# Expert values: order of the first loads, spread of the late vectors, and the final norm in PSUM

## The reference, cut to what matters

```python
def _layernorm(x, g, b):
    mu = jnp.mean(xf, axis=-1, keepdims=True)
    var = jnp.mean(jnp.square(xf - mu), axis=-1, keepdims=True)
    y = (xf - mu) * lax.rsqrt(var + NORM_EPS) * g + b
...
        expert = e1 * PEER_NKEYS + e2
        g = jax.nn.softmax(top_s)
        act = jax.nn.gelu(jnp.einsum('thkd,td->thk', u_tab[expert], ht))
        return jnp.einsum('thk,thkd->td', g * act, v_tab[expert])
...
        y_ff = _peer(h, ...)
        x = _layernorm(DEEPNORM_ALPHA * x + (1.0 + g2) * y_ff, ln2_g[l], ln2_b[l])
```

## Time and profile before

| what | us |
|---|---|
| median of three runs (1647.85 to 1650.1) | 1649.09 |
| the profiled execution | 1649.95 |
| its span in the profile | 1648.2 |
| PE busy | 1532.8 (93%) |
| DVE busy | 1287.7 (78%) |
| POOL busy | 957.5 (58%) |
| ACT busy | 686.8 (42%) |

### The profile page before, as it was taken

How to read it: one execution, slowest core, us unless ns; L and a number is a source line. 1 busy time by engine, 2 the same in 40 slices (tenths; PEclk the granted TensorE clock), 3 DMA queues, 4 the chain that set the end, 5 groups by cost and what they waited for, 6 DMA issues and landing times.

```text
span 1648.2 us, 21717 instructions
## 1 busy us (share of the span) xinstructions
PE 1532.8 (93%) x7951; PEld 1275.6 (77%) x7951; DVE 1287.7 (78%) x2005; ACT 686.8 (42%) x1270; POOL 957.5 (58%) x599
## 2 busy tenths in 40 slices
PE   6996898969999999997999999979899999999994
PEld 2344576437899999997999999957788888888883
DVE  5868731373139999999888899259799999999997
ACT  2030463104244343436888888323233333333340
POOL 2620000020026777785777788758789989989863
PEclk9997998989999999998999999989999999999997
DMA  9874206416015777785999999989999999999971
GB/s 369 313 212 52 29 1 213 132 51 204 1 49 172 261 262 263 263 309 196 369 351 380 354 361 378 393 295 360 381 378 379 365 383 372 383 369 377 367 253 51
DMA packets 217110, 438.91 MB, mean 266 GB/s; under 512 B 37156, under 2 KB 129828, under 8 KB 215212
## 3 DMA queue, kind: packets, MB, share of 16 engines
q1 hardware_dynamic: 179420, 302.44, 52.1%
q0 software_dynamic: 36864, 134.23, 22.5%
q10 hardware_dynamic: 720, 0.85, 0.2%
HBM read 379.66 MB, written 56.64 MB: 265 GB/s over the span
## 4 chain that ended last, share of the span: by engine, by line
PE 43%; DVE 18%; DMA 4%; issue 3%; POOL 1%; SPq 1%; ACT 0%; POOLq 0%; DVEq 0%; ACTq 0%
PE ps L1642 9%; PE ps L1643 9%; PE ps L1644 9%; PE ps L1618 5%; PE ps L1620 5%; PE ps L1619 4%; DVE junk L1700 2%; DMA a_in<-act_scr 2%; DMA v_raw<-in_peer_v 1%; PE ps L1633 1%; DVE cand L1737 1%; PE ps L1634 1%; DVE eq L1775 1%; DVE route L1776 1%; DVE idx L1735 1%
## 5 line engine op out<-in xcount | busy, mean ns | idle before, releaser
L1511 POOL TENSOR_TENSOR utl<-u_raw,uth 128x1024 fp32r<-128x1024 f32 x128 | 308.9, 2414 | 240.5 <-ACT uth L1528 238.6
L1618 PE MATMUL ps<-h2h,uth 128*128 128x384 f32 x1024 | 348.0, 340 | 0.2 <-POOL utl L1511 0.2
L1517 POOL TENSOR_TENSOR vl<-v_raw,vh 128x1024 fp32r<-128x1024 f32 x128 | 310.4, 2426 | 63.4 <-ACT vh L1528 61.5
L1620 PE MATMUL ps<-h2h,utl 128*128 128x384 f32 x1024 | 343.0, 335 | 0.0
L1619 PE MATMUL ps<-h2l,uth 128*128 128x384 f32 x1024 | 342.8, 335 | 0.0
L1642 PE MATMUL ps<-vh,wh 128*128 128x512 f32 x768 | 302.4, 394 | 17.9 <-DVE wl L1824 14.3
L1643 PE MATMUL ps<-vl,wh 128*128 128x512 f32 x768 | 301.3, 392 | 0.0
L1644 PE MATMUL ps<-vh,wl 128*128 128x512 f32 x768 | 301.0, 392 | 0.0
L1819 DVE TENSOR_TENSOR w_f<-a_in,g_in 128x384 f32<-128x384 f32 x128 | 231.7, 1811 | 55.5 <-DMA a_in<-act_scr 54.2
L1528 ACT ACTIVATE vh<-v_raw 128x1024 fp32r<-128x1024 f32 x128 | 135.3, 1057 | 198.2 <-DMA v_raw<-in_peer_v 182.4
L1618 PEld LDWEIGHTS ps<-h2h,uth 128*128 128x128 f32 x1024 | 192.9, 188 | 0.5 <-POOL utl L1511 0.5
(11 more groups left out here) (352 smaller groups left out, 2250.8 us busy)
## 6 DMA issues: line engine op xcount, KB each, us to landing
u_raw<-in_peer_uT SPq DMA_DIRECT2D x128, 512.0 KB
v_raw<-in_peer_v SPq DMA_DIRECT2D x128, 512.0 KB
w_ada<-in_w_ada SPq DMA_DIRECT2D x12, 2048.0 KB, 13.3
act_scr<-acts SPq DMA_DIRECT2D x64, 384.0 KB
g_scr<-stage SPq DMA_DIRECT2D x12, 2048.0 KB
g_in<-g_scr SPq DMA_DIRECT2D x32, 768.0 KB
...
```

The source lines that it names most:

```text
L1511: tt(k.utl[b % 3][:, :, :].rearrange(f3), k.u_raw[:, b % 4].rearrange(f3), k.uth[b % 3][:, :, :].bitcast(F32).rearrange(f3), ALU.subtract) ...
L1517: tt(k.vl[:, n % 4], k.v_raw[:, n % 4], k.vh[:, n % 4].bitcast(F32), ALU.subtract).then_inc(k.vl_done, 1)
L1618: mm(o, hi, k.h2h[:, kt, SP:T], start=(kt == 0), stop=False)
L1620: ins = mm(o, lo, k.h2h[:, kt, SP:T], start=False, stop=(kt == DK - 1))
```

## The change

Four things. (1) SP's list at the seam of the two stages: the loads of v blocks 0 and 1 stand in front of the load of u block 127 and of the store of activations 122/123; the second `g_in` stands behind v block 3; the last store of activations (`store_acts(63)`) stands behind the loads of v blocks 4 and 5; from there on each `g_in` is loaded one pair of blocks earlier. (2) `gate2`, `ln2_g`, `ln2_b` and the four tiles of `x1b` are seven loads of 512 KB, after v blocks 33, 41, 49, 57, 65, 73 and 81. (3) The skip and the statistics work in place in PSUM, by halves of 512 columns; those of token tile 0 stand on DVE among v blocks 126 and 127. PE's last four blocks go half by half for the last two tiles and tell each half (`y_done`). (4) For tiles 0 to 2 ACT applies mean and scale from PSUM to `y`, POOL multiplies by `ln2_g` and adds `ln2_b`; tile 3 is finished on DVE in three passes and stored in two halves.

```diff
@@ experts, k.block.sync @@
-        def load_ag(p):
+        def load_g(q):
+            sp.dma_start(k.g_in[:, q % 2]..., k.g_scr[:, :, 4 * q:4 * q + 4]...).then_inc(g_loaded[q % 2], 16)
+
+        def load_a(p):
             if p >= 2:
                 sp.wait_ge(k.w_done, 2 * p - 2)
-            if p % 2 == 0:
-                q = p // 2
-                sp.dma_start(k.g_in[:, q % 2]...)
+                if p % 2 and p < NBLK // 2 - 1:
+                    load_g((p + 1) // 2)
...
-            if b % 2:
+            if b % 2 and b < NBLK - 1:
                 store_acts(b // 2)
             if b in STORE_AT:
                 store_g(STORE_AT[b])
+            if b == NBLK - 6:
+                sp.wait_ge(k.g_out, GROUPS4)
+                load_v(0)
+                load_v(1)
             if b == NBLK - 5:
                 for c in range(2):
                     sp.wait_ge(g_stored[c], 16 * (NCH // 2))
-                sp.wait_ge(k.g_out, GROUPS4)
-                scr = k.mod_scr
-                for p in range(2):
-                    load_ag(p)
-                    load_v(2 * p)
-                    load_v(2 * p + 1)
+                load_g(0)
+                load_a(0)
+                load_v(2)
+                load_a(1)
+                load_v(3)
+                load_g(1)
...
         for p in range(2, NBLK // 2):
-            load_ag(p)
+            load_a(p)
             load_v(2 * p)
             load_v(2 * p + 1)
-            if p == 8:
-                sp.dma_start(k.gate2[:, :], ...).then_inc(s_gate2, 16)
-                sp.wait_ge(k.act_out, NBLK)
-                for name, dst in (("ln2_g", k.ln2_g), ("ln2_b", k.ln2_b)):
-                    sp.dma_start(dst[:, :], ...).then_inc(k.s_ln2, 16)
-                sp.wait_ge(k.s_x1out, 16 * TT)
-                sp.dma_start(k.x1b[:, :, :], ...).then_inc(k.s_x1b, 16)
+            if p == 2:
+                store_acts(NBLK // 2 - 1)
+            elif p == 16:
+                load_vector(k.gate2, ...)
+            elif p == 20:
+                load_vector(k.ln2_g, ...)
+            elif p == 24:
+                load_vector(k.ln2_b, ...)
+            elif p >= 28 and p % 4 == 0 and p < 28 + 4 * TT:
+                t = p // 4 - 7
+                sp.dma_start(k.x1b[:, t], k.x1_scr[t * P:(t + 1) * P, :]).then_inc(k.s_x1b, 16)
@@ k.block.gpsimd @@
-        for t in range(TT):
+        for t in range(TT - 1):
             pool.wait_ge(k.y_norm, t + 1)
+            tt(k.y[:, t], k.y[:, t], k.ln2_g[:, :], ALU.mult).then_inc(k.y_gain, 1)
+            pool.wait_ge(k.y_gain, t + 1)
             tt(k.y[:, t], k.y[:, t], k.ln2_b[:, :], ALU.add).then_inc(k.y_ready, 1)
@@ k.block.scalar @@
             nc.scalar.activation(k.rstd2[:, t:t + 1], k.mv2[:, t, 1:2], ACT.Sqrt, ...).then_inc(k.ln_sq, 1)
+            if t < TT - 1:
+                act.wait_ge(k.nmu2_ready, t + 1)
+                nc.scalar.activation(k.y[:, t], y_at[t], ACT.Identity, scale=k.rstd2[:, t:t + 1],
+                                     bias=k.nmu2[:, t:t + 1]).then_inc(k.y_norm, 1)
@@ k.block.vector @@
+        def add_skip(t, half):
+            y = y_at[t][:, cols]
+            if t:
+                dve.wait_ge(k.y_done, 2 * t - 1 + half)
+            step(tt(y, y, k.gate2[:, cols], ALU.mult))
+            step(v.scalar_tensor_tensor(y, k.x1b[:, t, cols], ALPHA, y, ALU.mult, ALU.add))
+            step(v.bn_stats(k.stats2[:, t, half], y))
+        def centre(t):
+            step.tell(v.bn_aggr(k.mv2[:, t], ...), k.rt1, TT + t + 1)
+        def normal(t):
+            dve.wait_ge(k.ln_sq, TT + t + 1)
+            step(v.reciprocal(k.rstd2[:, t:t + 1], k.rstd2[:, t:t + 1]))
+            v.tensor_scalar(k.nmu2[:, t:t + 1], k.mv2[:, t, 0:1], k.rstd2[:, t:t + 1], -1.0, ...).then_inc(k.nmu2_ready, 1)
...
+            if n >= NBLK - 2:
+                add_skip(0, n - NBLK + 2)
         split_w_low(NBLK - 1)
-        for t in range(TT):
-            stats(t)
-            if t:
-                normalise(t - 1)
-        normalise(TT - 1)
+        centre(0)
+        for t in range(1, TT):
+            add_skip(t, 0)
+            normal(t - 1)
+            add_skip(t, 1)
+            centre(t)
+        v.scalar_tensor_tensor(y, y, k.mv2[:, last, 0:1], k.ln2_g[:, :], ALU.subtract, ALU.mult)...
+        step(v.reciprocal(k.rstd2[:, last:], k.rstd2[:, last:]))
+        for half in range(2):
+            v.scalar_tensor_tensor(k.y[:, last, cols], y[:, cols], k.rstd2[:, last:], k.ln2_b[:, cols],
+                                   ALU.mult, ALU.add).then_inc(k.y_last, 1)
```

More of the change, by code:

```diff
@@ L1671, in _ @@
                     pe.wait_ge(k.gelu_done, NBLK)
[L1672 removed]
+                values(n, t, 0)
+                ins = values(n, t, 1)
             ins.then_inc(k.y_mm, 1)
[L1674 to L1680 removed]
+        for n in range(LAST4, NBLK):
+            pe.wait_ge(k.wl_done, n + 1)
+            pe.wait_ge(k.vl_done, n + 1)
+            values(n, 0, 0)
+            ins = values(n, 0, 1)
+        ins.then_inc(k.y_done, 2)
+        for t in range(1, DT):
+            for half in range(2):
+                for n in range(LAST4, NBLK):
+                    ins = values(n, t, half)
+                ins.then_inc(k.y_done, 1)
     @k.block.vector
@@ new lines, in _ @@
+        last = TT - 1
+        y = y_at[last]
+        v.scalar_tensor_tensor(y, y, k.mv2[:, last, 0:1], k.ln2_g[:, :], ALU.subtract, ALU.mult).then_inc(k.y_turned, 1)
+        dve.wait_ge(k.ln_sq, TT + last + 1)
+        step(v.reciprocal(k.rstd2[:, last:], k.rstd2[:, last:]))
+        dve.wait_ge(k.y_turned, 1)
+        for half in range(2):
+            cols = slice(half * 512, (half + 1) * 512)
+            v.scalar_tensor_tensor(k.y[:, last, cols], y[:, cols], k.rstd2[:, last:], k.ln2_b[:, cols],
+                                   ALU.mult, ALU.add).then_inc(k.y_last, 1)
```

80 lines of the change are left out of this document (30 added, 50 removed).

## The result

The changed kernel takes 1623.87 us (median of four runs, 1622.26 to 1628.11); the kernel before took 1648.47 beside it (1646.59 to 1650.1). The ratio is 0.985, with a 95% interval of 0.9827 to 0.9873. The forecast was 1626.5. The profiled execution took 1628.11 us, the longest of the four; the prediction made its sum of 1627.35 for an execution of this kind.

The account below looks back on a forecast made before the run. PE was taken as full from 1200 to 1600 us, so only the time before and behind could shrink: 1649.95 - 11.3 (middle) - 11.3 (tail) = 1627.35, lowered to 1626.5 because the profiled execution lay 0.86 above the median; range 1620 to 1636.

Parts of the forecast that it names:

- PE's end: Last matmul of the v stage: moves from 1624.7 to 1613.4 us, a gain of 11.3 us before the tail.
- The three waits at blocks 3 to 5: PE's early v waits for `wl`: all go with the earlier `a_in`, gaining 5.0 us; 1.3 if DVE sets the last two.
- The first v loads in front of u block 127: Seam: 2 to 3 us wait for the last `utl`, nearly cancelled; cost 0.5 us, bounds -1.5 and +5.
- The late vectors: Vector loads in the v stage: spreading removes a 7.3 us stall and half clock, costs 0.5 us against the lead.
- The seam: Between u and v stages: 5.0 us from three waits removed, less 0.5 for the early v loads.
- The lead: DVE's `wl` ahead of PE in the v stage: about 5 us at block 33, under 2 at block 81.
- Tile 0's passes in front of the last `wl`: DVE's work among the last v blocks: tile 0 done early except its mean, no PE wait priced.
- The tail: From PE's end to the span's end: 12.2 us instead of 23.5, gain 11.3, bounds 8 and 13, POOL last.
- The price of nothing for POOL's work beside passes in PSUM: Final norm: DVE's in-place PSUM passes are not slowed by POOL; otherwise the tail is 3.5 us longer.
- The stream as the bound: Rival, v stage: DMA engines can't deliver faster, the middle gains 6.8 instead of 11.3 us, 1631; chance 0.20.
- The late u block: Rival, seam: two v loads delay the last u block by more than 5 us, half clock follows, 1631; chance 0.12.
- The slower case: Rival, v stage: each vector stops PE and lowers the clock; gain gone at 3.2 us a vector; chance 0.03.

Follow-up runs that it names:

- e5: The kernel before with one edit: the store waiting for gelu(127) moved behind the loads of v blocks 4 and 5; 1636.82 us, ratio 0.9934.
- e9: The changed kernel with the old load order at the seam and each `g_in` before its own pair, only `store_acts(63)` still moved; 1627.95 us, ratio 0.9876.
- e2: The kernel before with only the seven late vector loads spread over blocks 33 to 81; 1646.42 us, ratio 0.9982.
- e4: The changed kernel run again without edits, beside its separate parts; 1624.48 us, ratio 0.9864.
- e1: The kernel before with only the changed norm and tail, old list of loads; 1637.09 us, ratio 0.9940.
- e3: The kernel before with only the new seam load order and earlier `g_in`, vectors in one piece behind block 17; 1640.05 us, ratio 0.9943.
- e10: The changed kernel with all seven vector loads in one piece behind v block 57; 1629.42 us, ratio 0.9888.
- e7: The changed kernel with the passes of the skip and norm writing to `y` in SBUF instead of PSUM; 1632.39 us, ratio 0.9902.
- e11: The changed kernel with the seven vector loads 16 blocks apart, after v blocks 17 to 113; 1626.14 us, ratio 0.9871.
- e6: The changed kernel with gelu(127) on ACT in front of the splits of v blocks 2 and 3; 1621.52 us, ratio 0.9844.
- e8: The changed kernel without POOL's addition of `ln2_b` for tiles 0 to 2; 1622.02 us, ratio 0.9843.
- e12: The changed kernel with the old seam list except the moved store, gelu(127) first, and vector loads 16 blocks apart; 1623.59 us, ratio 0.9862.

## Why the prediction was right, point by point

**PE's end** (forecast 1613.4, measured 1613.85). From the first v matmul to E the kernel before took 544.1 us for 521.9 us of matmuls, the changed one 532.5: 22.3 lost before, 10.6 after. With the first v matmul 0.8 us later (1081.36 against 1080.57) that makes the 10.85 by which E moved. Term by term, from the two profiles: 5.0 (three waits) + 7.3 (vectors) - 0.8 (later start) - 1.2 (gelu(127), 4.78 against 3.62) - 3.2 (waits at the end) + 3.6 (less half clock at the seam). The last three were not in the forecast's sum and nearly cancel, so that E was hit within half a microsecond is in part luck; the other profile of the same kernel has E at 1608.0. And the priced terms were not right one by one:

- *The three waits at blocks 3 to 5* (5.0): gone, as said. The store is what did it (e5), and the `a_in` was issued 1.4 us after the forecast time.
- *The first v loads in front of u block 127* (-0.5): the waits came where they were put (2.96 and 0.34), and the first v matmul lost 0.8. The bounds of -1.5 and +5 were much too wide; in e9 the waits at the seam sum to much the same. The half clock cost less, which no term had: taking the waits, with 0.16 for each, from the 22.3 and 10.6 us lost leaves 8.1 us before and 2.5 now, 1.9 of the difference at the vectors. The 1.6 us in u block 127 are in the later start.
- *The late vectors* (7.3 - 0.5): **mis-sized as a term of its own**. Alone they gave 2.7 (e2), on top of the other parts 3.5 (e4 less e1 and e3), against one piece behind block 57 4 to 6 (e10).
- *The seam* as a term was mis-sized the other way: 9.1 (e3) and 11.1 (e5) where 4.5 was forecast.

Both errors have one main source. I took the two stalls as independent. They draw on one account, the lead: at block 16, ahead of the vectors, the moved store raises it from 3.7 to 7.3 us (e5), which also covers two thirds of the vectors' stall (1.66 + 0.56 + 0.32 = 2.5 of 7.3 us are left); and without it the spread loads meet a lead that they use up. The rest of the seam's excess is the half clock. The sum of the parts came out at 23.8 against a forecast of 22.6 all the same, since what one term had too much the other had too little: right in the sum, not in the pricing.

**The lead** was forecast at 5 at block 33 and under 2 at block 81; the rows give 7.5 and 3.3. The fall between them, 4.2 us, is less than the 7.1 that I worked out.

**Tile 0's passes in front of the last `wl`**: the prediction put nothing on them. That step failed in the first profile. Between wl(126) and wl(127) stand 2.1 us of tile 0, and PE waited 1.01 + 0.16 for wl(127), 1.83 + 0.16 for wl(126): 3.2 us. Ten profiles have these passes. In four PE waits there (the first, e7, e9, e11), with a lead of 0.9 to 1.8 at block 120; in six it doesn't (e1, e4, e6, e8, e10, e12), with 1.1 to 3.4. What parts them is how many of DVE's passes between w_f(125) and wl(126) take over 2.5 us, beside one of POOL's: three in each of the four, two in each of the six. That is read from the rows; no run took the meetings away.

**The tail** (forecast 12.2, measured 12.45; alone, in e1, 12.0 of gain by the median and 11.1 by the profile, for 11.3). DVE's half passes cost 0.70 instead of 0.68, POOL was last as said, at E + 8.0 instead of E + 7.6. The price of nothing for POOL's work beside passes in PSUM held: 686 to 700 ns for the eight L1861, 695 to 697 for the eight L1862. e7 shows the other side. The Trainium skill, page "SBUF — State Buffer", section "SBUF: two separate sides", has GpSimd and a DVE pass with two SBUF inputs exclude each other, and the trace agrees: L1862 in SBUF takes up to 2.39 us in e7, POOL's last add 3.20.

**The rivals.** The stream as the bound (1631) didn't come in the changed kernel: PE stood full from 1200 to 1598, at 0.98 of DMA share. In e2, e9 and e11, where the lead is gone sooner, a small form of it did. The late u block cost 2.96 us, not over 5. The slower case needed 3.2 us of stall per vector; in both profiles of the changed kernel the seven loads of 512 KB caused no wait of PE at all (e7, with the same list, has 0.34 and 0.69 us at blocks 83 and 94). The Trainium skill's advice to batch to 1 MiB or more (page "DMA: Bandwidth & Descriptors", section "Measured") speaks for the one load of 2 MB that `x1b` was before. The trace shows no loss by the split: 383 GB/s from 1200 to 1400 us with the vectors in it, 375 before without them. That section measures DMAs issued from GpSimd, and these are issued by SP. e10 doesn't test it, for its seven loads are of 512 KB too.

**Open.** Why the DMA engines are less busy from 1400 to 1600 us (0.92 and 335 GB/s, against 1.05 and 383 from 1200 to 1400) while DVE waits for `a_in` six times (seven times from 1200 to 1400). What lowers e9's lead between blocks 20 and 24. And the spread between executions: PE comes to u block 127 at 1074.99 in one profile of the changed kernel and at 1071.66 in the other, in stages that no edit touches; medians of four to six runs can't tell 2 us apart here.
